# A decoder layer on one core: TensorE's four loops written out, and the wait of the even heads' first output products lowered by one value quarter

## What is computed

```
z = x @ w_in + b_in                    # GLU input | q latent | kv latent | rope key | gates
y_conv = silu(LN(dwconv31(a * sigmoid(g)))) @ w_conv_out
q_lat, q_rope = absorbed / rotated queries of 8 heads;  c_kv, k_rope = latent and rotary key
prompt: softmax(causal(q_lat.c_kv + q_rope.k_rope)) . c_kv, then w_uv  (here: keys and values per head)
sample: the same over 4096 cached positions per sample (paged) and the 4 new ones
mix = (g_conv * y_conv + g_mla * (v @ w_mla_out)) @ w_mix_out
x1 = LN(alpha * x + mix)
f = (silu(hg) * hv) @ w_down,  [hg | hv] = dwconv3(x1 @ w_up)    # D_FF = 2816
y = LN(alpha * x1 + f)
```

## Time and profile before

| what | value |
| --- | --- |
| median of 3 runs | 2126.86 us (2125.67 to 2131.3) |
| the profiled execution's own time | 2125.47 us |
| its span (first to last instruction) | 2123.3 us |
| TensorE busy with matmuls | 2043.9 us, 96% of the span, 13579 matmuls |
| VectorE, ScalarE, GpSimd busy | 1277.0, 662.7, 572.2 us |
| chain that ended last, share of TensorE | 85% |
| "issue" in that chain | 3% |

### The profile page before, as it was taken

One profiled execution on the slowest core, in us unless ns is written; L12 is line 12 of the kernel. 1 busy time (PEld: TensorE's weight loads), 2 busy tenths in 40 slices (PEclk: granted clock), 3 DMA queues, 4 the chain that ended last, 5 costly groups with the idle time before them and its releaser, 6 DMA issues.

```text
span 2123.3 us, 34518 instructions
## 1 busy us (share of the span) xinstructions
PE 2043.9 (96%) x13579; PEld 1936.8 (91%) x13579; DVE 1277.0 (60%) x1768; ACT 662.7 (31%) x1114; POOL 572.2 (27%) x292
## 2 busy tenths in 40 slices
PE   8999999999989999989999999999999999999997
PEld 7999999998988888866669998999999999999996
DVE  2999999944657667654444326654545453545457
ACT  4222222234234444443341115322222121222223
POOL 4722433302110000124311256312131212131314
PEclk9999999999999999999999999999999999999998
DMA  6422332216310011145735431111111111111112
GB/s 205 154 91 71 105 103 81 90 51 228 116 43 11 15 25 30 40 184 210 281 119 172 119 101 51 50 41 51 40 50 40 51 40 51 40 50 41 50 58 98
DMA packets 162524, 183.07 MB, mean 86 GB/s; under 512 B 19852, under 2 KB 135366, under 8 KB 158260
## 3 DMA queue, kind: packets, MB, share of 16 engines
q1 hardware_dynamic: 144581, 108.28, 17.1%
q0 software_dynamic: 8320, 46.27, 5.7%
q10 hardware_dynamic: 9505, 26.77, 3.4%
HBM read 150.21 MB, written 31.93 MB: 86 GB/s over the span
## 4 chain that ended last, share of the span: by engine, by line
PE 85%; DVE 6%; issue 3%; ACT 3%; DMA 1%; POOL 1%; ACTq 0%; SPq 0%; DVEq 0%
PE psa L2207 26%; PE psb L2207 26%; PE psb L2848 5%; PE psa L2848 5%; PE psb L2396 4%; PE psa L2396 4%; PE psb L2647 1%; PE pst L2626 1%; PE psa L2594 1%; PE psb L2594 1%; DVE ptl L1745 1%; PE pst L2469 1%; DVE nmx L1729 1%; PE pst L2629 1%; DMA xrow<-in_x_prompt 1%
## 5 line engine op out<-in xcount | busy, mean ns | idle before, releaser
L1489 POOL TENSOR_TENSOR wlo<-wraw,whi 128x1024 fp32r<-128x1024 f32 x64 | 172.3, 2707 | 567.8 <-ACT whi L1246 567.8
L1569 DVE SCALAR_TENSOR_TENSOR pst<-g_ext,wtap,pst 128x512 f32<-128x512 f32 x464 | 306.9, 747 | 0.0
L1339 POOL TENSOR_TENSOR wlo<-wraw,whi 128x1024 fp32r<-128x1024 f32 x64 | 155.0, 2428 | 386.7 <-ACT whi L750 290.1
L2040 DVE TENSOR_SCALAR hg<-ueg,fwv,vec 128x1024 f32<-128x1024 f32 x22 | 19.3, 876 | 243.4 <-ACT ueg L1271 235.8
L2207 PE MATMUL psa<-x1h,whi 128*128 128x352 f32 x504 | 109.6, 326 | 3.3 <-issue 3.3
L2207 PE MATMUL psa<-x1h,wlo 128*128 128x352 f32 x504 | 109.0, 324 | 2.0 <-issue 2.0
L2207 PE MATMUL psb<-x1h,whi 128*128 128x352 f32 x504 | 109.0, 324 | 0.0
L2207 PE MATMUL psb<-x1h,wlo 128*128 128x352 f32 x504 | 108.6, 323 | 0.0
L2207 PE MATMUL psb<-x1l,whi 128*128 128x352 f32 x504 | 108.5, 323 | 0.0
L2207 PE MATMUL psa<-x1l,whi 128*128 128x352 f32 x504 | 108.5, 323 | 0.0
L2043 DVE SCALAR_TENSOR_TENSOR hg<-ueg,fwv,hg 128x1024 f32<-128x1024 f32 x44 | 97.3, 2212 | 5.7 <-DVE hg L2040 0.2
(11 more groups left out here) (537 smaller groups left out, 5355.0 us busy)
## 6 DMA issues: line engine op xcount, KB each, us to landing
wraw<-in_w_up SPq DMA_DIRECT2D x44, 512.0 KB, 3.7
wraw<-in_w_in SPq DMA_DIRECT2D x37, 512.0 KB, 3.8
wraw<-in_w_down SPq DMA_DIRECT2D x22, 512.0 KB, 3.7
xt_d<-tmp POOLq DMA_DIRECT2D x8, 528.0 KB, 3.4
gb_d<-stg ACTq DMA_DIRECT2D x8, 528.0 KB, 2.6
ga_d<-stg ACTq DMA_DIRECT2D x8, 528.0 KB, 3.8
ma_d<-stg ACTq DMA_DIRECT2D x8, 528.0 KB, 2.9
tmp<-gb_d SPq DMA_DIRECT2D x8, 528.0 KB, 3.7
```

The source lines that it names most:

```text
L1339: nc.gpsimd.tensor_tensor(wlo[:, n % HL, :], wraw[:, n % RAW, :], whi[:, n % HL, :].bitcast(F32), ALU.subtract).then_inc(lo_done, 1)
L1489: nc.gpsimd.tensor_tensor(wlo[:, (ns + 2) % HL, :], wraw[:, (ns + 2) % RAW, :], whi[:, (ns + 2) % HL, :].bitcast(F32), ALU.subtract).then_ ...
L1569: half[x] = link(nc.vector.scalar_tensor_tensor(out=dst, in0=src, scalar=tap(k_), in1=pst[:, x, :], op0=ALU.mult, op1=ALU.add))
```

## The change

The four loops of TensorE's program (and of no other engine) become loops of the script that writes the program: their bodies stand one behind the other, with the counts of the waits as constants. And for a_ = 0 `pe_out` waits for three value quarters of its pair and not four; for a_ = 1 it waits for four, as before.

```diff
-            with pe.Fori(CSUM, MT) as m:
+            for m in range(CSUM, MT):
                 in_products(m, 1)
...
                 if a_ < 2:
-                    pe.wait_ge(v_lo, 4 * i2 + 4)
+                    pe.wait_ge(v_lo, 4 * i2 + (3 + a_))
                     pe.wait_ge(o_read, 4 * h + 2)
...
-            with pe.Fori(1, H // 2 - 1) as i:
+            for i in range(1, H // 2 - 1):
                 for s in range(2):
                     pe_head(2 * i + s, s, True, i)
...
-            with pe.Fori(0, NB // 2 - 1) as i:
+            for i in range(0, NB // 2 - 1):
                 pe_sample(2 * i + 1, 1, i)
                 pe_sample(2 * i + 2, 0, i + 1)
...
-            with pe.Fori(0, PAIRS) as i:
+            for i in range(PAIRS):
                 for s in range(2):
                     pe_ffn((i, s))
```

## The result

The changed kernel takes 2104.03 us in the median (2103.19 to 2104.11, 4 runs); the kernel before, beside it, 2127.51 (2125.67 to 2131.3, 4 runs). The ratio is 0.9886, with a 95% interval of 0.9869 to 0.9904: faster by 1.1%. The forecast was 2104.0. The profiled execution after is the one of 2103.19 us; its span is 2101.0, against 2123.3 before, so 22.3 us went.

The account below looks back on a forecast made before the run. TensorE, busy 96% of the span, bounds the kernel, so only its idle or slow time can be won. 15.2 + 7.1 = 22.3 us off gave 2103.2 (profiled execution) or 2104.6 (median); forecast 2104, range 2099.6 to 2111.

Parts of the forecast that it names:

- Part one: Even heads' first output product waits for three value quarters, not four: 15.2 us won in all (bounds 7.0, 18.2).
- rival 1: Even heads: clock falls behind a new wait, about 1 us, before the second output product; 4.8 us given back; 8%.
- Part two: Feed-forward loop written out: gaps at its back edges go, 1.79 us each, 7.1 in all (bounds 5.3, 8.8).
- Part three: Loops of input products, heads and samples written out, register instructions gone: 0 us taken, samples between 0 and 2.0.
- Rival 4: Three earlier loops written out: about 24 more fetched packets each stall TensorE, 43 us lost, time 2147; 2%.

Follow-up runs that it names:

- The wait alone: Only the wait lowered against the kernel before, TensorE's four loops kept: 2130.52 us, ratio 0.9941.
- the moved quarter: Changed kernel with VectorE's fourth value quarter moved behind the scaling of row 4: first 2119.65 us, ratio 0.9888; again, on another chip, 2099.64 us, ratio 0.9871.

## Why the prediction was right, point by point

- **The time**, 2104.0, against 2104.03. The agreement to 0.03 us is partly luck: the sum gave 2103.2 off the profiled execution and 2104.6 off the median, 2104 was chosen between them, and four things that it did not count (start 1.4 and samples 1.0 won, head 7's clock 1.3 and the tail 1.17 lost) cancel.
- **Part one**, 15.2. Measured 15.04: 3.58, 3.60, 3.92 and 3.94 where 3.54, 3.71, 4.01 and 3.96 stood. The hinge was right: the maximum of row 5 starts 0.80 behind the last value instruction (0.82 forecast), and the second output product 3.33 behind that (3.33 and 3.36). An even head takes 41.86 (41.7 forecast). The wait alone gave the same windows, so it is shown that this part does not need the loops written out.
- **The new wait** that rival 1 named was there, 0.92 us, and the clock did not fall behind it; the rival's 4.8 us did not come. That it can fall behind a wait, of 2.56 us, is seen in head 7, in six of ten traces (last section).
- **Part two**, 7.1. Measured 7.34 in the changed kernel, and some 7 in the medians with this loop alone written out. The number was right because it was taken from the gaps themselves; the 0.2 us that it missed is mostly the exit: the loop's window now is 1.51 us longer than five passes of 139.84, and 1.66 was put. Its cause, as the prediction put it, was not: it read rows 8 as a matter of how long a body is. A loop of the same 864 matmuls branched in 208 ns, and this loop did once 50 instructions had been put ahead of it.
- **The rule from the Trainium skill**, "Runtime: NRT & Kernel Launch", section on instruction fetch mechanics, that a taken branch out of the two pages at hand forces a fetch: the runs show passes that touch 7 pieces of 16 KB and branch in 208 ns with no fetch at all, so what is at hand is more than two. The same section gives TensorE 128 KiB, which is eight blocks of 16 KiB. The runs agree with that figure, if one of the eight is always the block fetched ahead; that last part is inferred and was not tried by itself.
- **Part three**, 0 with an upper bound of 2.0. Measured 0.95 for the samples, in three traces against three; the sum had put it at 0 because TensorE's own part hardly differed. The heads' and the input products' loops gave nothing that a window shows.
- **Rival 4** (each newly fetched block stalls TensorE) is out. 11 packets more came in the run as a whole, 107 in place of 96, and no gap stands at any. The prediction had expected about 24 more; as it counted only the loops that got longer, it left out that the feed-forward part would fetch fewer, 33 in place of 43, since a slow branch fetches its first pieces again.

## What to carry to other kernels

Where a loop's branch is slow, look first at where its body lies: the times of the instruction queue's packets show the pieces, and two loops of one length can differ by 1.8 us per pass through place alone. Writing the loop out is the sturdy cure; a few instructions moved ahead of it are the cheap one, but any later edit ahead of the loop can undo it. When a wait is lowered, count to the next event on the other engine from which two known cases run alike (here the maximum of row 5), and not the length of the wait: it was 3.2 us, and 3.6 to 3.9 came back, since the clock stayed up behind it.

## What the hardware showed that was not expected

- Two loops of 864 matmuls in one kernel, with branches of 208 and 3327 ns; the slow one turned fast by a shift of 50 instructions, and of 40 (207 to 208 ns). With the pass lying in a third place a back edge lost 1.09 us, against 1.84.
- TensorE's increments of a semaphore, 51 ns each as a row, follow each other only every 0.15 us (50 of them from 1305.2 to 1312.7).
- The same 2.56 us wait in head 7 was followed by the full clock in the kernel before, and by a mean of 0.75 in 5 us just behind it in the changed one (row below). It is not the change: from this product to the next long wait it took 6.94 or 6.95 us in four traces (the kernel before, the wait alone, the changed kernel's second trace, the moved quarter's second) and 8.25 to 8.45 in the six others, among them the changed kernel's first. So one and the same kernel shows both; what tells two executions apart is open.

```profile
905.00:910.00 5.00, 4.83 (x33) 4.59 (x32) 1.03 (x3) 1.36 (x3) 0.00 (x0) 0.75 0.99 367
```

- VectorE's scaling of 128x512 elements takes 1.89 us in even heads and 2.41 in odd ones, though the same operation on 128x640 takes 0.55. Each time GpSimd has just begun an operation of its own (L1415), and the scaling ends 0.28 us after that one in each of heads 0 to 6. In head 7, where GpSimd has no such operation, the same scaling takes 0.49. This is the scaling that made the fourth quarter late in the first place. No run moved GpSimd's operation away, so that it is the cause rests on these eight heads and was not tried. The timelines of GpSimd, and of VectorE in heads 3 and 7:

```profile
695.86 2.40 POOL L1415 TENSOR_TENSOR wlo<-wraw,whi 128x1024 fp32r<-128x1024 f32 x1 [37.38 <-ACT whi L924]
733.41 3.81 POOL L1415 TENSOR_TENSOR wlo<-wraw,whi 128x1024 fp32r<-128x1024 f32 x2 [35.14 <-ACT whi L924]
```
```profile
733.67 2.41 DVE L1737 TENSOR_SCALAR pbuf<-pbuf,rr 128x512 f32<-128x512 f32 x1
737.52 0.55 DVE L1737 TENSOR_SCALAR pbuf<-pbuf,rr 128x640 f32<-128x640 f32 x1
...
891.02 0.49 DVE L1737 TENSOR_SCALAR pbuf<-pbuf,rr 128x512 f32<-128x512 f32 x1
```
